# The x mixers of a two-block model in fp32: convolution steps moved ahead, mLSTM decays run two steps ahead instead of one

## The chip, the cores and the metric

The kernel runs on one core of a Trainium2 chip, as one launch. The metric is the device time of one execution in microseconds. The kernel before was run three times: 2325.51, 2322.0 and 2324.71 us, median 2324.71. Engines are called as in the profile: PE (TensorE), DVE (VectorE), ACT (ScalarE), POOL (GpSimd) and SP (SyncE, which issues DMAs).

## What is computed

The reference is a model of two blocks on 256 tokens of width 1024, all in fp32. The first block has forgetting attention and retention, each followed by a mixture of 32 experts. The second block, to which the change belongs, has two layers. In each, a context of 256 tokens and the input x pass a mixer and a feed-forward network. The mixer projects the normed input once and cuts the result into three branches:

```
px = (rmsnorm(x, norm1_g[l]) * (1.0 + sc1) + sh1) @ w_in[l] + b_in[l]
# 1 bidirectional mLSTM, 4 heads of 128, chunks of 128 tokens: q, k, v, o and 16 gate columns
b = cumsum(fc); m_new = max(b_last + m, max(w_log)); decay = exp(b_last + m - m_new)
C_new = decay * C + einsum('bhsk,bhsv->bhkv', ks, vc)
num = w_inter * einsum('bhtk,bhkv->bhtv', qc, C) + einsum('bhts,bhsv->bhtv', s, vc)
h = num / max(abs(den), exp(-m_t))
# 2 chunk_sgu: gelu, layer norm of one half, a product over 128 tokens, times the other half
# 3 conformer_conv: y = a * sigmoid(g); depthwise convolution of 31 taps; layer norm; silu
x = x + g1 * (concat(y_a, y_b, y_c) @ w_out[l])
```

For x the convolution is axial: half of the 256 channels is convolved along rows of 64 tokens (31 taps), the other half along the 4 rows (7 of the taps can reach). Weights are split into a high and a low part, and each product takes three matmuls (high x high, high x low, low x high).

## The kernel before, in words

Every stage is written as one generator or function per engine (`pe`, `act`, `dve`, `pool`, `loads` for SP). Each engine runs its own list in the order written, and engines meet through counted semaphores only. No scheduler moves anything: the order of the work is the order of the code. The stages are attention, experts (with the context's first mixer beside them), retention, experts (with the context's feed-forward network and second mixer beside them), and then twice an x mixer (`x_mixer`, L3268) and an x feed-forward network, and the final norm.

**Items.** `Gemm` (L365) cuts a weight matrix into items of 128 x 1024 numbers. For each, SP loads a slot of the ring, ACT writes `high` (`act_high`, L433), DVE writes `low` (`dve_low`, L444), and PE runs the matmuls (L490). An x mixer has 26 items: two small ones for the gates, then two each for `conv_a`, `conv_g`, `sgu_u` and `sgu_v` (items 2 to 9), and four each for q, k, v and o (10 to 25). There are four pairs of `high` and `low`: ACT and DVE prepare item n + 4 while PE works on n. One 128x1024 low half is the row `DVE L444`.

**What lies between the items.** The generator `dve` (L2951) goes through the items in step (`proj.dve_paced`). From item 4 on it takes `rate` = 4 steps of side work after each low half: first the gate chain (`gate_chain`, L2725: 20 steps on 8 partitions, scans and maxima of the gates), and when that is exhausted the convolution (`conv`, L2781: 43 steps, being a memset, the product a*sigmoid(g), two copies into the padded `yt`, 31 row taps, 7 column taps and a final sum, L2831). In the first x mixer `settle` (L707) follows with nine steps that norm x itself (L710, L715). The SGU's steps on DVE stand after items 10, 11 and 19, its matmuls on PE (L2421, L2426) after item 19.

**The layer norm of the convolution** needs two sums over channels, made on PE with a matrix of ones (`conv_sum_pe`, L2412): one of the values, one of their squares. Between them DVE centres (L2839) and ACT squares (L2584). `ln_at` (L2346) is the item after which the first sum stands on all three engines; the second stands two items later. It is computed from the number of side steps and is 21 before.

**mLSTM.** After the items come four steps i = 0 to 3 (two directions of two chunks; `order`, L2348). For each: PE makes the decays (`decay_pe`) in PSUM, ACT takes their exponential into `wb` (L2602), DVE adds the mask (L2881), ACT takes exponentials of that in place (L2612), DVE multiplies q by `wb` into `qs` (L2894) and the scores by the weights into `mst` or a part of `tm` (L2898), and k into `ks` (L2907). Then `num` (PE L2457 and L2458, DVE L2915 to L2927: the denominators of two heads at a time, and the division) and `state` (PE L2471, DVE L2943), which multiplies the state by one column of `wb` and adds the new product. Numerators and state of step i stand `lag` = `deep` - 1 steps behind its decays; `deep` is 2 for the x mixers (L3270) and 1 for the context's. `deep` also is the number of buffers `wb`, `ks` and `qs`. `Turns` hands out buffers and banks in turn and keeps what frees each. The low halves of the first two items of the output projection stand ahead of the loop's last step (L3016).

Of the kernel before, what the change touches and what calls it, by code (L numbers as in the profile page):

```python
# [15 lines left out]
P = 128  # L16
# [124 lines left out]
def build(nc, A):  # L141
    ctx = ExitStack()
    with ctx:
# [2080 lines left out]
        def mixer(L, v, get, part, room, bk, opened, npairs, wide, rate, deep, early_in=None, x_ready=None, xx=None, rs=None, lender=None):  # L2224
# [42 lines left out]
            kn = part2("kn", 2, 4, P)  # L2267
            if v:
                mod = Modulation(name, room, [(1, 2 if L else 1)], 4 if L else 0, row=kn[:, 0].rearrange("p h d -> p (h d)"), cs=cs)
            wbs, kss = ([part2(n, 4, P) for _ in range(deep)] for n in ("wb", "ks"))  # L2270
            qs_t, st_t, ks_t, wb_t = None, None, Turns(kss, kept), Turns(wbs, kept)
            if not states_only:
                hn = part2("hn", 2, 512)
                qss, sts = [part2("qs", 4, P) for _ in range(deep)], [part2("mst", 4, P)]
                if deep > 1:
                    sts.append(tf[:, 1024:1536].rearrange("p (h t) -> p h t", h=4))
                rd = part2("rd", 4)
                st2.close()
                if v:
                    pairs2 = pairs  # L2280
                    st1.close()
                else:
                    st3, part3 = part()
                    pairs2 = pair_buffers(part3, npairs)
                    st3.close()
                qs_t, st_t = Turns(qss, kept), Turns(sts, kept)
# [56 lines left out]
            x_done = lambda c: [(ev_v, outp.out(0, wide * (c // per), c % per))]  # L2343
            early = Early(f"ffn{L}{v}", xs, T, [ut[:, 0, :], ut[:, 1, :]], x_done) if v else None
            conv_ops, conv_end = 0 if states_only else 43 if v else 65, K("taps") if v else (K("conv"), 65)
            ln_at = (ends["gate"] + 3 + -(-(20 + conv_ops) // rate)) // 2 * 2 + 1  # L2346
            sgu_at, sgu_lag = None if states_only else ends["sgu_v"] + 1, 9 if v else 3
            order = [(0, 0), (1, 1), (0, 1), (1, 0)]  # L2348
            lag = deep - 1
# [534 lines left out]
            def prelude_dve(dve, i):  # L2884
                d, a = order[i]
                le = P - 1 if d == 0 else 0
                s0, s1 = a * P, (a + 1) * P
                dt, wb = dts[i % 2], wb_t[K(i)]
                if i in outs:
                    qs, st = qs_t.next(K(i)), st_t.next(K(i))  # L2890
                    for s, k in qs_t.freed(K(i)):
                        dve.wait_ge(*s.at(k))
                    dve.wait_ge(*pl_a.at(K(i, 1)))
                    dve.tensor_tensor(qs, qt[:, :, s0:s1], wb, MUL).then_inc(*qs_v.up(K(i)))  # L2894
                    wb_t.free(K(i), (qs_v, K(i)))
                    dve.wait_ge(*ms_p.at(K(i)))
                    dve.wait_ge(*pd_a.at(K(i, 1)))
                    dve.tensor_tensor(st, bk[K("mscore", i)][:, :].rearrange("p (h t) -> p h t", h=4), dt, MUL).then_inc(*ms_v.up(K(i)))  # L2898
                    bk.free(K("mscore", i), (ms_v, K(i)))
                if i not in final:  # L2900
                    ks = ks_t.next(K(i))
                    for s, k in ks_t.freed(K(i)):
                        dve.wait_ge(*s.at(k))
                    dve.wait_ge(*pd_a.at(K(i, 1)))
                    if i < 2:
                        dve.wait_ge(*kn_a.at(K(1)))
                    dve.tensor_tensor(ks, kn[:, a], bc(dt[:, :, le], [P, 4, P], 2), MUL).then_inc(*ks_v.up(K(i)))  # L2907

            def num_dve(dve, i, hp):
                d, a = order[i]  # L2910
                pv = bk[K("num", i, hp)][:, 0:258].rearrange("p (h n) -> p h n", h=2)
                em = emt[:, 8 * d + 4 * a + 2 * hp:8 * d + 4 * a + 2 * hp + 2]
                seq = in_order(dve, v_step, K("den", i, hp))
                dve.wait_ge(*mo_p.at(K(i, hp)))
                seq(dve.tensor_copy(rd[:, 2:4], pv[:, :, 128]))  # L2915
                if i < 2:
                    dve.wait_ge(*gt_a.at(K(1, "m")))
                seq(dve.scalar_tensor_tensor(rd[:, 0:2], rd[:, 2:4], -1.0, em, MUL, MAX))
                seq(dve.tensor_tensor(rd[:, 0:2], rd[:, 0:2], rd[:, 2:4], MAX))
                seq(dve.reciprocal(rd[:, 0:2], rd[:, 0:2]))  # L2920
                for j in range(2):
                    h = 2 * hp + j
                    o = hn[:, a, h * P:(h + 1) * P]
                    if i >= 2:
                        n = dve.scalar_tensor_tensor(o, pv[:, j, 0:P], rd[:, j:j + 1], o, MUL, ADD)
                    else:
                        n = dve.tensor_scalar(o, pv[:, j, 0:P], rd[:, j:j + 1], None, MUL)  # L2927
                n.then_inc(*mo_v.up(K(i, hp)))
                dve.wait_ge(*mo_v.at(K(i, hp)))
                bk.free(K("num", i, hp), (mo_v, K(i, hp)))  # L2930

            def state_dve(dve, i, hp):
                d, a = order[i]
                le = P - 1 if d == 0 else 0
                wb = wb_t[K(i)]
                pv = bk[K("state", i, hp)][:, 0:258].rearrange("p (h n) -> p h n", h=2)
                dve.wait_ge(*mc_p.at(K(i, hp)))
                dve.wait_ge(*pl_a.at(K(i, hp)))
                if i < 2 and hp == 0:
                    dve.wait_ge(*cn_v.at(state_before(i)))  # L2940
                for j in range(2):
                    h = 2 * hp + j
                    n = dve.scalar_tensor_tensor(cn[:, d, h, :], cn[:, d, h, :], wb[:, h, le:le + 1], pv[:, j, :], MUL, ADD)  # L2943
                n.then_inc(*cn_v.up(K(i, hp)))
                bk.free(K("state", i, hp), (cn_v, K(i, hp)))
                if hp:
                    wb_t.free(K(i), (cn_v, K(i, 1)))

            sq4 = None if states_only else [qss[0], sts[0]]
# [1 line left out]
            def dve(dve):  # L2951
# [21 lines left out]
                    yield  # L2973
                    yield from norm_turns(lambda part: norm.split_dve(dve, None, part))
                yield
                chains, taps = gate_chain(dve), iter(())
                for it in proj.dve_paced(dve):
                    if it is None:
                        yield
# [2 lines left out]
                    if mod and L and at == 6:  # L2982
                        mod.out_dve(dve, 1, 2)
                    if at > ends["gate"] + 2:
                        for _ in range(rate):
                            if chains is not None and next(chains, True):
                                chains, taps = None, iter(()) if states_only else conv(dve)
                            if chains is None and next(taps, True):
                                next(settle, None)
                    if not states_only:  # L2990
# [6 lines left out]
                        if at in (ln_at, ln_at + 2):  # L2997
                            conv_ln_dve(dve, (at - ln_at) // 2)
                    yield
                run(chains or taps)  # L3000
                run(settle)
                for which in late():
                    conv_ln_dve(dve, which)
# [263 lines left out]

        def x_mixer(L, before, opened, early_in, x_ready):  # L3268
            room = Room(f"mix{L}", 8, before, opened)
            early, x_done, s = mixer(L, 1, room, room.part, room, banks, opened, 4, 512, 4, 2, early_in, x_ready)  # L3270
            room.close()
            return room, early, x_done, in_one_go(s)

# [242 lines left out]
```

## Time and profile before

| | |
|---|---|
| median of 3 runs | 2324.71 us |
| the profiled execution | 2330.65 us |
| its span in the profile | 2328.7 us |
| mean granted clock of PE | 0.955 |
| PE busy | 2133.0 us, 92% |
| DVE busy | 1118.6 us, 48% |
| ACT busy | 870.9 us, 37% |
| DMA | 676.24 MB, mean 290 GB/s |

The profiled execution is one more run, 5.9 us above the median; 2.0 us of it lie outside the span. Everything read from the trace is on the clock of its span. Busy shares are means over stages with different limits, so the change is read where it happens: the first x mixer's projections end near 1689 us and its mLSTM near 1723 us, the second's near 2054 and 2088 us. A wait in brackets is idle time of the engine just before the instruction, with what ended it.

### The profile page before, as it was taken

The page shows a single profiled execution, that of the slowest core. Times are in us where ns is not written, and L with a number is a line of the kernel's source. Part 1 is how long each engine was busy: PE and PEld are TensorE (multiplying, and loading weights), DVE is VectorE, ACT ScalarE, POOL GpSimd, SP SyncE. Part 2 cuts the span into 40 slices and gives each one's busy share as a digit, 9 for nine tenths or more (in the row PEclk, how much of TensorE's full clock was granted, in tenths as well). Part 3 has the DMA queues.
Part 4 walks back from the last instruction along what each step waited for, and adds up shares of the span by engine and source line. Part 5 has one row for each costly group of instructions (what it writes and reads, how often), then busy time and mean ns, then how long its engine had stood idle before and what let it go on. Part 6 is the DMA issues. An engine that isn't in the chain of part 4 may idle for free. (4 is left out here: it accounts for less than half of the span.)

```text
span 2328.7 us, 44642 instructions
## 1 busy us (share of the span) xinstructions
PE 2133.0 (92%) x19242; PEld 1728.9 (74%) x19242; DVE 1118.6 (48%) x1956; ACT 870.9 (37%) x1473; POOL 83.7 (4%) x160
## 2 busy tenths in 40 slices
PE   7998889998786999989999998977989999988999
PEld 7967556665553987967777776636878998878999
DVE  5455326533523743543433335324865545765554
ACT  4434233243212443332322222324444444554443
POOL 0000000000000000001010110000000000000001
PEclk9989999999998999999999999998989999988999
DMA  8567999999999568599999999897426556513550
GB/s 296 163 236 282 382 412 417 381 387 425 424 426 374 177 227 302 212 383 417 409 391 408 422 411 376 358 412 285 157 92 247 185 166 210 179 55 135 184 177 31
DMA packets 128078, 676.24 MB, mean 290 GB/s; under 512 B 11488, under 2 KB 11744, under 8 KB 65920
## 3 DMA queue, kind: packets, MB, share of 16 engines
q1 hardware_dynamic: 111616, 614.77, 67.8%
q0 software_dynamic: 16256, 58.50, 6.6%
q8 instruction: 157, 2.57, 0.4%
q14 instruction: 49, 0.40, 0.0%
HBM read 672.17 MB, written 1.05 MB: 289 GB/s over the span
## 5 line engine op out<-in xcount | busy, mean ns | idle before, releaser
L490 PE MATMUL bank<-xx,high 128*128 128x256 f32 (+1 forms) x3296 | 630.8, 293 | 30.2 <-DVE xx L653 13.7
L490 PEld LDWEIGHTS bank<-xx,high 128*128 128x128 f32 (+1 forms) x3296 | 518.5, 194 | 90.5 <-issue 61.3
L490 PE MATMUL bank<-xx,low 128*128 128x256 f32 (+1 forms) x1648 | 473.4, 287 | 0.0
L490 PEld LDWEIGHTS bank<-xx,low 128*128 128x128 f32 (+1 forms) x1648 | 319.9, 194 | 1.0
L444 DVE TENSOR_TENSOR low<-lane,high 128x1024 fp32r<-128x1024 f32 (+1 forms) x112 | 130.7, 1170 | 256.6 <-ACT high L433 256.4
L433 ACT ACTIVATE high<-lane 128x1024 fp32r<-128x1024 f32 (+1 forms) x112 | 113.1, 1013 | 288.0 <-PE bank L490 284.1
L490 PE MATMUL bank<-hx,high 128*128 128x256 f32 x1056 | 197.4, 288 | 0.0
L490 PEld LDWEIGHTS bank<-hx,high 128*128 128x128 f32 x1056 | 163.9, 191 | 18.1 <-issue 16.0
L490 PE MATMUL bank<-hx,low 128*128 128x256 f32 x528 | 149.2, 283 | 0.0
L490 PE MATMUL bank<-gth,high 128*128 128x256 f32 x384 | 112.9, 294 | 6.6 <-DVE gtl L651 5.2
L1484 ACT ACTIVATE hs<-bank 64x256 f32<-64x256 f32 x64 | 24.1, 377 | 246.6 <-PE bank L1471 246.2
L490 PE MATMUL bank<-gth,low 128*128 128x256 f32 x384 | 110.7, 288 | 0.0
L490 PE MATMUL bank<-gtl,high 128*128 128x256 f32 x384 | 110.6, 288 | 0.0
L490 PE MATMUL bank<-high,xx 128*128 128x256 f32 (+1 forms) x416 | 103.9, 330 | 0.7 <-DVE tm L2839 0.7
L1491 DVE TENSOR_TENSOR hs<-hs,bank 64x256 f32<-64x256 f32 x64 | 27.1, 423 | 154.9 <-ACT hs L1484 154.5
L490 PEld LDWEIGHTS bank<-hx,low 128*128 128x128 f32 x528 | 101.0, 191 | 0.0
L490 PEld LDWEIGHTS bank<-gth,high 128*128 128x128 f32 x384 | 75.7, 197 | 13.3 <-DVE low L444 7.2
L1540 DVE COPY y<-bank 128x256 f32<-128x256 f32 x64 | 27.1, 423 | 121.5 <-PE bank L1525 121.1
L444 DVE TENSOR_TENSOR low<-ring__14,high 128x1024 fp32r<-128x1024 f32 x50 | 60.8, 1222 | 50.5 <-ACT high L433 50.2
L490 PEld LDWEIGHTS bank<-high,xx 128*128 128x128 f32 x416 | 71.4, 191 | 17.5 <-issue 8.8
L490 PE MATMUL bank<-xh,high 128*128 128x256 f32 x256 | 74.8, 292 | 7.0 <-DVE low L444 3.5
L1552 PE MATMUL bank<-tmp,y 32*128 32x256 f32 x1024 | 78.9, 424 | 1.5 <-DVEq L1641 1.1
(602 smaller groups left out, 3977.4 us busy)
## 6 DMA issues: line engine op xcount, KB each, us to landing
ring__13<-in_expert_gu_blocks SPq DMA_DIRECT2D x36, 1024.0 KB, 10.4
ring__14<-in_expert_gu_blocks SPq DMA_DIRECT2D x35, 1024.0 KB, 9.6
ring__15<-in_expert_gu_blocks SPq DMA_DIRECT2D x35, 1024.0 KB, 9.8
lane<-in_w_gu_blocks POOLq DMA_DIRECT2D x44, 512.0 KB, 8.5
ring__47<-in_expert_gu_blocks SPq DMA_DIRECT2D x18, 1024.0 KB, 11.9
ring__159<-in_expert_gu_blocks SPq DMA_DIRECT2D x18, 1024.0 KB, 9.6
ring__160<-in_expert_gu_blocks SPq DMA_DIRECT2D x18, 1024.0 KB, 9.3
ring__158<-in_expert_gu_blocks SPq DMA_DIRECT2D x18, 1024.0 KB, 9.8
```

Source lines behind the costliest of these rows:

```text
L433: act.activation(self.split_parts(it)[0].bitcast(F32R), src, ACT.Copy).then_inc(*hi.up(it["key"]))
L444: dve.tensor_tensor(low.bitcast(F32R), src, high, SUB).then_inc(*lo.up(it["key"]))
L490: done = pe.matmul(out, a.bitcast(F32R), b.bitcast(F32R), start=it["start"] and k == 0 and q == 0 and (not halves or u == it["outs"][0]), ...
L1484: act.activation(hs[0:64, :], pq[K("up", b)][0:64, 0:256], ACT.Silu).then_inc(*up_a.up(K(b)))
L1491: dve.tensor_tensor(hs[0:64, :], hs[0:64, :], pq[K("up", b)][64:128, 0:256], MUL).then_inc(*up_v.up(K(b)))
L1540: dve.tensor_copy(y, pq[key][:, 0:256]).then_inc(*dn_v.up(K(b)))
L1552: i = pe.matmul(acc_b[h][:, j * T:(j + 1) * T], y[32 * h:32 * h + 32, j * P:(j + 1) * P], d[32 * h:32 * h + 32, b % GB, :], start=False, s ...
```

## The change

Two things, both in `mixer`, for the x mixers (v = 1).

**The convolution starts beside the gate chain.** As soon as item 5, the last of `conv_g`, is past, every second one of DVE's four side steps is followed by one convolution step, though the gate chain isn't through. Six convolution steps so come before item 9 instead of from item 9 on. `ln_at` is computed with the six steps taken off and becomes 19: the two sums stand after items 19 and 21.

**The decays run two steps ahead.** `deep` is 3 and `lag` 2. There are three `qs` and three places for the weighted scores (the third is a part of `tm`, which the SGU no longer needs by then), but still two `wb` and two `ks`. For steps 0 and 1 the last column of `wb` is copied to a small `wle` right after `qs` is made; the state update reads `wle`, and `wb` is free after the copy. In all mixers, the context's too, the denominators aren't copied from PSUM any more; the two steps behind read them there.

```diff
-            wbs, kss = ([part2(n, 4, P) for _ in range(deep)] for n in ("wb", "ks"))
+            wbs, kss = ([part2(n, 4, P) for _ in range(min(deep, 2))] for n in ("wb", "ks"))
+            wle = part2("wle", 2, 4) if v else None
...
-                    sts.append(tf[:, 1024:1536].rearrange("p (h t) -> p h t", h=4))
+                    sts += [tf[:, z:z + 512].rearrange("p (h t) -> p h t", h=4) for z in (1024, 1536)]
...
-            ln_at = (ends["gate"] + 3 + -(-(20 + conv_ops) // rate)) // 2 * 2 + 1
+            early_taps = 2 * (ends["gate"] + 3 + 20 // rate - ends["conv_g"] - 1) if v else 0
+            ln_at = (ends["gate"] + 3 + -(-(20 + conv_ops - early_taps) // rate)) // 2 * 2 + 1
...
                     wb_t.free(K(i), (qs_v, K(i)))
+                    if v and i not in final:
+                        dve.tensor_copy(wle[:, i, :], wb[:, :, le]).then_inc(*qs_v.up(K(i, "last")))
+                        wb_t.free(K(i), (qs_v, K(i, "last")))
...
-                seq(dve.tensor_copy(rd[:, 2:4], pv[:, :, 128]))
...
-                seq(dve.scalar_tensor_tensor(rd[:, 0:2], rd[:, 2:4], -1.0, em, MUL, MAX))
-                seq(dve.tensor_tensor(rd[:, 0:2], rd[:, 0:2], rd[:, 2:4], MAX))
+                seq(dve.scalar_tensor_tensor(rd[:, 0:2], pv[:, :, 128], -1.0, em, MUL, MAX))
+                seq(dve.tensor_tensor(rd[:, 0:2], rd[:, 0:2], pv[:, :, 128], MAX))
...
-                dve.wait_ge(*pl_a.at(K(i, hp)))
+                dve.wait_ge(*(qs_v.at(K(i, "last")) if v else pl_a.at(K(i, hp))))
...
-                    n = dve.scalar_tensor_tensor(cn[:, d, h, :], cn[:, d, h, :], wb[:, h, le:le + 1], pv[:, j, :], MUL, ADD)
+                    n = dve.scalar_tensor_tensor(cn[:, d, h, :], cn[:, d, h, :], wle[:, i, h:h + 1] if v else wb[:, h, le:le + 1], pv[:, j, :], MUL, ADD)
...
-                if hp:
+                if hp and not v:
                     wb_t.free(K(i), (cn_v, K(i, 1)))
...
-                chains, taps = gate_chain(dve), iter(())
+                chains, taps = gate_chain(dve), conv(dve) if v else iter(())
...
-                        for _ in range(rate):
-                            if chains is not None and next(chains, True):
-                                chains, taps = None, iter(()) if states_only else conv(dve)
+                        for n in range(rate):
+                            if chains is not None:
+                                if next(chains, True):
+                                    chains, taps = None, taps if v else iter(()) if states_only else conv(dve)
+                                elif v and at > ends["conv_g"] and n % 2:
+                                    next(taps)
...
-            early, x_done, s = mixer(L, 1, room, room.part, room, banks, opened, 4, 512, 4, 2, early_in, x_ready)
+            early, x_done, s = mixer(L, 1, room, room.part, room, banks, opened, 4, 512, 4, 3, early_in, x_ready)
```

In the rows below, line numbers of the changed kernel are two to eight higher, and ring buffers have other numbers.

The first sum of the layer norm on PE, second x mixer, before: L493 is the bias that closes a group of v, L2412 the sum.

```order
L490 MATMUL bank<-high,xx 128x512
L493 MATMUL bank<-row,ones_r 128x512
L2412 MATMUL bank<-tm,vec 128x256 x2
L490 MATMUL bank<-high,xx 128x512
L490 MATMUL bank<-low,xx 128x512
L490 MATMUL bank<-high,xx 128x512 x2
```

And now: L2428 are the last matmuls of the SGU, L2414 is the sum.

```order
L2423 MATMUL bank<-row,vec 64x256 x2
L2428 MATMUL bank<-wst,tm 64x128 x4
L2423 MATMUL bank<-row,vec 64x256 x2
L2428 MATMUL bank<-wst,tm 64x128 x4
L2414 MATMUL bank<-tm,vec 128x256 x2
L490 MATMUL bank<-high,xx 128x512
L490 MATMUL bank<-low,xx 128x512
```

The sum stood behind the last v item; now it stands right behind the SGU's matmuls, with the last two v items still to come.

The end of the convolution on DVE, second x mixer, before: L444 are the low halves of items 22 and 23, L2814 and L2825 taps, L2831 the final sum, L2872 the SGU's product.

```order
L2814 SCALAR_TENSOR_TENSOR tm<-yt,vec,tm 128x256
L444 TENSOR_TENSOR low<-ring__301,high 128x1024
L2814 SCALAR_TENSOR_TENSOR hn<-yt,vec,hn 128x256
L2814 SCALAR_TENSOR_TENSOR tm<-yt,vec,tm 128x256
L2831 TENSOR_TENSOR tm<-tm,hn 128x256
L2872 TENSOR_TENSOR yt<-tm,bank 128x256 x2
L444 TENSOR_TENSOR low<-ring__300,high 128x1024 x2
L2839 SCALAR_TENSOR_TENSOR tm<-bank,tm 128x256 x2
L2844 RECIPROCAL rs<-rs 128x256
L2846 TENSOR_TENSOR tm<-tm,rs 128x512
```

And now, with L2833 as the final sum, ring__303 for items 22 and 23, and L2841 as the centring:

```order
L2816 SCALAR_TENSOR_TENSOR hn<-yt,vec,hn 128x256
L2816 SCALAR_TENSOR_TENSOR tm<-yt,vec,tm 128x256
L2816 SCALAR_TENSOR_TENSOR hn<-yt,vec,hn 128x256
L2816 SCALAR_TENSOR_TENSOR tm<-yt,vec,tm 128x256
L444 TENSOR_TENSOR low<-ring__303,high 128x1024
L2833 TENSOR_TENSOR tm<-tm,hn 128x256
L444 TENSOR_TENSOR low<-ring__303,high 128x1024
L2874 TENSOR_TENSOR yt<-tm,bank 128x256 x2
L2841 SCALAR_TENSOR_TENSOR tm<-bank,tm 128x256 x2
L444 TENSOR_TENSOR low<-ring__302,high 128x1024 x2
```

The final sum stands behind the low half of item 22 instead of item 23, and the centring ahead of the low half of item 24.

The second half of the mLSTM's step 1 on DVE, second x mixer, before: `rd` are the denominators.

```order
L2881 TENSOR_TENSOR tm<-bank,vec 128x256 x2
L2894 TENSOR_TENSOR qs<-qt,wb 128x512
L2898 TENSOR_TENSOR tm<-bank,tm 128x512
L2907 TENSOR_TENSOR ks<-kn,tm 128x512
L2915 COPY rd<-bank 128x2
L2918 SCALAR_TENSOR_TENSOR rd<-rd,rs 128x2
L2919 TENSOR_TENSOR rd<-rd 128x2
L2920 RECIPROCAL rd<-rd 128x2
```

And now:

```order
L2883 TENSOR_TENSOR tm<-bank,vec 128x256 x2
L2896 TENSOR_TENSOR qs<-qt,wb 128x512
L2899 COPY wle<-wb 128x4
L2903 TENSOR_TENSOR tm<-bank,tm 128x512
L2912 TENSOR_TENSOR ks<-kn,tm 128x512
L2883 TENSOR_TENSOR tm<-bank,vec 128x256 x2
L2896 TENSOR_TENSOR qs<-qt,wb 128x512
L2903 TENSOR_TENSOR tm<-bank,tm 128x512
L2922 SCALAR_TENSOR_TENSOR rd<-bank,rs 128x2
```

The mask and products of step 2 (L2883, L2896, L2903) stand between those of step 1 and the numerators of step 0, and the copy ahead of the denominators is gone.

## Rows read from the trace of the kernel before

**Rows 1.** The page, its line on PE: busy us (share) and instructions.

```profile
PE 2133.0 (92%) x19242; PEld 1728.9 (74%) x19242; DVE 1118.6 (48%) x1956; ACT 870.9 (37%) x1473; POOL 83.7 (4%) x160
```

**Rows 2.** Table of stretches: length, busy us per engine, PE clock, DMA share, GB/s.

```profile
1626.00:1671.00 45.00, 44.74 (x321) 39.88 (x320) 42.72 (x85) 23.27 (x32) 0.00 (x0) 1.00 0.51 165
1680.85:1684.26 3.41, 3.41 (x10) 2.66 (x9) 1.88 (x2) 1.76 (x2) 0.00 (x0) 0.50 0.27 109
1695.25:1723.18 27.93, 23.23 (x149) 21.69 (x149) 23.65 (x77) 12.49 (x30) 0.00 (x0) 0.83 0.07 18
1994.20:2039.53 45.33, 44.52 (x324) 39.46 (x322) 43.10 (x88) 23.10 (x31) 0.00 (x0) 1.00 0.53 166
2059.83:2087.76 27.93, 23.02 (x148) 21.57 (x147) 23.60 (x77) 12.49 (x30) 0.00 (x0) 0.82 0.07 19
```

**Rows 3.** Timeline of PE, first x mixer: start, us, what [wait before <- releaser].

```profile
1664.03 0.66 PE L2426 MATMUL bank<-wst,tm 128*64 128x128 f32 x8
...
1671.36 1.13 PE L2412 MATMUL bank<-tm,vec 128*128 128x256 f32 x4
...
1680.29 1.51 PE L2412 MATMUL bank<-tm,vec 128*128 128x256 f32 x4 [2.34 <-ACT tm L2584]
```

**Rows 4.** Timeline of PE, second x mixer.

```profile
2019.29 0.51 PE L490 MATMUL bank<-xx,high 128*128 128x256 f32 x2 [0.81 <-DVE low L444]
...
2032.49 0.66 PE L2426 MATMUL bank<-wst,tm 128*64 128x128 f32 x8
...
2039.91 1.13 PE L2412 MATMUL bank<-tm,vec 128*128 128x256 f32 x4
...
2046.47 1.02 PE L2412 MATMUL bank<-tm,vec 128*128 128x256 f32 x4
```

**Rows 5.** Timeline of DVE, second x mixer, projections.

```profile
1994.20 1.23 DVE L444 TENSOR_TENSOR low<-ring__300,high 128x1024 fp32r<-128x1024 f32 x1 [5.40 <-ACT high L433]
...
2005.94 0.91 DVE L2787 MEMSET yt<- 128x1016 f32 x1 [0.16 <-issue]
...
2012.99 1.23 DVE L444 TENSOR_TENSOR low<-ring__14,high 128x1024 fp32r<-128x1024 f32 x1 [1.31 <-ACT high L433]
...
2018.02 1.22 DVE L444 TENSOR_TENSOR low<-ring__15,high 128x1024 fp32r<-128x1024 f32 x1
2019.15 0.48 DVE L2825 SCALAR_TENSOR_TENSOR tm<-yt,vec,tm 128x256 f32<-128x256 f32 x1
2019.55 0.48 DVE L2814 SCALAR_TENSOR_TENSOR hn<-yt,vec,hn 128x256 f32<-128x256 f32 x1
...
2039.10 0.43 DVE L2831 TENSOR_TENSOR tm<-tm,hn 128x256 f32<-128x256 f32 x1
```

**Rows 6.** Timeline of DVE, first x mixer, the convolution's end and what follows.

```profile
1670.69 0.42 DVE L2831 TENSOR_TENSOR tm<-tm,hn 128x256 f32<-128x256 f32 x1
1671.03 1.75 DVE L710 RECIPROCAL on<-on 128x256 f32<-128x256 f32 x1
...
1674.43 1.67 DVE L715 SCALAR_TENSOR_TENSOR xr<-xr,vec,on 128x256 f32<-128x256 f32 x4
...
1678.73 0.74 DVE L2839 SCALAR_TENSOR_TENSOR tm<-bank,tm 128x256 f32<-128x256 f32 x2
```

**Rows 7.** Timeline of DVE, second x mixer, mLSTM.

```profile
2061.66 0.69 DVE L2898 TENSOR_TENSOR mst<-bank,tm 128x512 f32<-128x512 f32 x1 [0.48 <-ACT tm L2612]
...
2065.91 0.15 DVE L2915 COPY rd<-bank 128x2 f32<-128x2 f32 x1
2066.10 0.16 DVE L2918 SCALAR_TENSOR_TENSOR rd<-rd,rs 128x2 f32<-128x2 f32 x1
...
2070.39 0.76 DVE L2881 TENSOR_TENSOR tm<-bank,vec 128x256 f32<-128x256 f32 x2 [0.50 <-ACT wb L2602]
```

**Rows 8.** Timeline of PE behind the mLSTM, first and second x mixer.

```profile
1719.32 0.51 PE L490 MATMUL bank<-xx,high 128*128 128x256 f32 x2 [0.47 <-DVE low L444]
...
2091.93 0.63 PE L2557 MATMUL bank<-vec,hn 128*128 128x128 f32 x4 [2.11 <-DVE hn L3051]
```

More of the change, by code:

```diff
@@ L2934, in state_dve @@
                 le = P - 1 if d == 0 else 0
-                wb = wb_t[K(i)]
+                wb = None if v else wb_t[K(i)]
                 pv = bk[K("state", i, hp)][:, 0:258].rearrange("p (h n) -> p h n", h=2)
                 dve.wait_ge(*mc_p.at(K(i, hp)))
-                dve.wait_ge(*pl_a.at(K(i, hp)))
+                dve.wait_ge(*(qs_v.at(K(i, "last")) if v else pl_a.at(K(i, hp))))
                 if i < 2 and hp == 0:
@@ L2999, in dve @@
                     yield
-                run(chains or taps)
+                run(chains or ())
+                run(taps)
                 run(settle)
```

## The prediction

> **What bounds the kernel now.** I read the page's head first. PE is busy for 92% of the span, so a wait removed elsewhere pays only where PE was standing for it [rows 1]. The change touches the two x mixers. The table of stretches separates two phases in each of them, together 73 of the 2329 us. In the projections PE is busy 44.7 of 45.0 us and 44.5 of 45.3 us, DVE 42.7 and 43.1: both engines are full at once, PE ahead by a hair. In the mLSTM stretches (27.9 us each) PE is busy 23 us, DVE 23.6, the clock is granted at 0.82, and DVE's order sets the end [rows 2].
>
> Then PE's timeline, to see where it stood. In the first mixer it waited 2.34 us for the second sum of the convolution's layer norm at 1680.29 [rows 3]; right behind that the granted clock was 0.5 for 3.41 us [rows 2], which cost half of it, 1.7 us. In the second mixer it waited 0.81 us at 2019.29, and neither of the two sums (L2412) shows a wait [rows 4]. So the second mixer's projections have almost nothing to give.
>
> DVE's timeline shows why. In the second mixer it is idle for 5.40 us before 1994.20, which is before the convolution's inputs exist, then only 0.16 us before the memset and 1.31 us before 2012.99 until the convolution ends at 2039.10 + 0.43 = 2039.53 [rows 5]. PE's first sum starts 0.38 us later, at 2039.91 [rows 4]. In the first mixer the same pair is 1671.11 and 1671.36 [rows 3, 6]. The end of the convolution already meets the sum.
>
> **Part 1, the convolution beside the gate chain.** Nothing is added or removed on DVE. Six of the 43 steps (memset, product, two copies, two taps) move ahead of three low halves, and everything behind runs six steps earlier in items. But DVE is already full there, so its clock time hardly moves. Of the work ahead of the convolution's end only one low half drops out (the last but two in the projections): 1.13 us by the spacing 2018.02 to 2019.15 [rows 5]. Besides, the memset's 0.16 us goes, and steps put between dependent gate steps overlap: dependent ones start 0.04 us after the end of the one before (2065.91 to 2066.10, with 0.15 us of work) [rows 7], independent ones 0.09 us before it (2018.02 to 2019.15, with 1.22 us of work) [rows 5]. Some four crossings at 0.13 us give 0.5, with the memset's 0.16 about 0.6 (bounds 0 and 1.2). So the end of the convolution comes 1.7 us earlier: 2037.8 and 1669.4. The 1.31 us stays, since ACT still has to wait for DVE's statistics.
>
> On PE the sums move two items forward, from item 21 to 19 and from 23 to 21. Two items that stood ahead of the first sum now stand behind it: from the end of the SGU matmuls to the sum, 2039.91 - (2032.49 + 0.66) = 6.76 us, in the first mixer 1671.36 - (1664.03 + 0.66) = 6.67 us [rows 3, 4]. Second mixer: the sum starts 2.1 us earlier with 6.76 us more behind it, so the projections end 6.76 - 2.1 = 4.7 us later. First mixer: 6.67 - 1.95 = 4.7 us later, less the 2.34 us wait and the 1.7 us of slow clock, since the second sum's input is then ready: convolution end 1669.4, plus one low half (1.1), the reciprocal (1.7), six steps of L715 (2.4), the gated product and the centring (0.7 each) and ACT's square (0.7 with its hand-over), 7.3 us [rows 5, 6], gives 1676.7, and PE is there at 1669.4 + 0.8 + 6.7 = 1676.9. Rest 4.7 - 4.0 = 0.7 us.
>
> Where does the wait show? Six taps of 0.40 us now precede the low half of item 16, less 0.6: it lands 1.8 us late, PE starts that item at 2021.1 instead of 2019.3, and it reaches the first sum at 2033.15 + 1.8 = 2034.95, where it stands 2.85 us (first mixer: 1666.4 to 1669.4, 3.0 us). Waits of 2 to 3 us can cost clock, as the 2.34 us one did; the 0.81 us one did not. A drop at the first of the two waits is absorbed by the second, one at the second is paid. Between 0 and 1.7 us in each mixer, 3.4 if it lasts twice as long; I take 0.8, for two 1.6.
>
> **Part 2, decays two steps ahead.** In each mixer DVE waits twice 0.50 us for ACT's `wb`, which waits for the buffer that the state update still reads [rows 7]; the copied column frees it, and the decay matmuls now stand ahead of the numerators on PE. Gain 1.0 us. The waits of 0.48 us for ACT's exponentials (four per mixer) stay, as DVE still has only the `qs` product between asking and needing. The two new copies (like L2915, 0.15 us) fall into these waits: cost 0; 0.3 if not. The copy of the denominators goes: eight times 0.19 us by the spacing of 2065.91 and 2066.10, 1.5 us [rows 7]. Sum 2.5 us per mixer (bounds 1.0 and 2.9).
>
> Does PE see it? In the second mixer its transposes wait 2.11 us for `hn` [rows 8], so yes. In the first they wait for nothing, but follow two output items and the modulation; those items start on the low halves at 1719.32 with 0.47 us of waiting [rows 8], and these low halves move from behind numerator 2 to ahead of it, so they come more than 2.5 us earlier. Yes there too. Two mixers: -5.0 us.
>
> The two steps that replace the denominators' copy now read PSUM. The row of such a read is 0.15 us, of the same size from SBUF 0.16 us [rows 7]: I add nothing, and 0.02 us each for 16 is the bound, 0.3 per mixer. The Trainium skill (VectorE: DVE Perf Modes, "Rules for kernel authors") says to copy out of PSUM first if many steps follow, and its table in the section on the TRN2 errata gives 120 cycles fixed for a PSUM source against 58 for SBUF. At its 0.96 GHz that is an estimate of 65 ns more on each of the 16 steps, 1.0 us per mixer, and by it the total would be 2.0 us slower. The rows speak against it: at 128x2 the PSUM read is the shorter.
>
> In the context mixer, beside the experts, the same eight copies go; DVE is not what that stage waits for, and I count 0.
>
> **Sum.** First mixer +0.7 - 2.5, second +4.7 - 2.5, clock +1.6: +2.0 us. The profiled execution took 2330.65 us; it becomes 2332.7. The median of the runs is 5.9 us below that execution, and 2324.71 + 2.0 = 2326.7 us.
>
> **Rivals.** The measurement tells apart about 0.2%, 4.65 us.
> (a) Forecast: the two parts nearly cancel; from -3 to +4.6 us. 56%.
> (b) The clock pays. Both waits at the first sum are followed by one or two spells of 0.5, 1.7 to 3.4 us each instead of 0.8, and the mLSTM keeps only 2 us per mixer: 5.4 + 3.4 to 6.8 - 4 = +4.8 to +8.2, 2331 to 2332. For it: the 2.34 us wait did so. Against: a first drop absorbs into the wait that follows. 25%.
> (c) Faster. The convolution's end comes as early as PE does. It decides at 3 us: the gate chain would have to hide the six steps in its own dependencies, so that the low halves are not late and the end moves from 1.7 to 5 us earlier. Then the second mixer's projections stay as they were, the first loses its 4.0 us, and with 5.0 from the mLSTM it is -9, 2315.7 us. For it: gate steps are on 8 partitions and short; against it: they start 0.04 us behind each other, there is no room. Half of that shift gives -4.5. With both 13%.
> (d) Part 2 does not do what it says: a bank or buffer wait stands in for `wb`, only the denominators' copies are gained, 1.5 per mixer, less with slower PSUM reads. +2.0 + 2.0 to +4.0, 2329 to 2331. For it: eight banks now serve one more step in flight. Against it: each bank asked for was read a whole step earlier. 6%.
>
> **How the numbers follow.** Faster by over 0.2%: (c) less its nearer half, 0.11. Slower: (b), half of (d) and the upper tail of (a), 0.31. Within 0.2%: 0.58. The range leaves out the end of (c) and the top of (b): 2318.5 to 2332.5; that of (a) alone is 2321.7 to 2329.3.
>
> **What would show it.** Right: PE idle of some 3 us ahead of the first layer-norm sum in both mixers, released by DVE's last convolution step; PE idle of 2 us at item 16; no wait at the second sum; DVE's end of convolution only 1 to 2 us earlier from the start of the projections; no wait for `wb` at decays 2 and 3, 25.4 us instead of 27.9 for the mLSTM on DVE. Wrong: a first sum without a wait (then (c)), short steps on PSUM above 0.2 us, or DVE idle in the gate stretch.

## The result, and the profile after

The changed kernel took 2329.35 us (median of 15 runs) against 2323.42 us for the kernel before (15 runs on the same chip): a ratio of 1.0021, 95% interval 1.0014 to 1.0029, so +3.3 to +6.7 us. (Each kernel had one far slower run, 2428.99 and 3356.71 us; the ratio is over the others, while the medians, over all runs, are 5.9 us apart.) A second comparison, on another occasion (below, the changed kernel again), gave 1.0014 (1.0004 to 1.0024). The forecast was +2.0 us, 2326.7 us: the right side of zero, but below the first interval. The change is slower, by about as much as a measurement can just tell.

The profiled execution after took 2324.49 us, with a span of 2322.7 us. That is shorter than the profiled execution before, though the medians stand the other way: the stages ahead of the x mixers, which the change hardly touches, differed by 8.7 us between the two executions (the x mixers start at 1630.8 us before and at 1622.1 after). So below only stretches between fixed points are compared, and from the start of the first x mixer's SGU projections to the end of the span it is 697.9 us before and 700.6 after.

The page's line on engines, to be read against [rows 1]: eight copies in each x mixer and eight more in the context's are gone, and four new ones are there (DVE has 1936 instructions where it had 1956). PE has the same instructions.

```profile
PE 2122.5 (91%) x19242; PEld 1723.4 (74%) x19242; DVE 1113.9 (48%) x1936; ACT 870.6 (37%) x1473; POOL 83.9 (4%) x160
```

The table below has, in us and from the timelines, what the stretches of the x mixers took, and what lies behind them. "Projections" runs from PE's first bias matmul of `sgu_v` to its first transpose of k, "mLSTM" from there to the first transpose of `hn`.

| | before | after | forecast |
|---|---|---|---|
| projections, first x mixer | 59.41 | 61.87 | +0.7, and clock |
| mLSTM, first | 38.58 | 34.46 | -2.5 |
| projections, second x mixer | 55.76 | 62.10 | +4.7, and clock |
| mLSTM, second | 37.10 | 34.35 | -2.5 |
| behind the first mLSTM, up to the second mixer's projections | 270.2 | 269.6 | nothing |
| behind the second mLSTM, up to the end of the span | 236.8 | 238.1 | nothing |
| end of the convolution after item 10's low half | 43.03 and 43.34 | 41.49 and 41.79 | -1.7 |

PE's timeline after, first x mixer (start, us, what, and in brackets the wait before it and its releaser), answers to [rows 3]:

```profile
1639.30 0.50 PE L490 MATMUL bank<-xx,high 128*128 128x256 f32 x2 [1.00 <-ACT qt L2301]
...
1644.27 0.50 PE L490 MATMUL bank<-xx,high 128*128 128x256 f32 x2 [1.12 <-DVE low L444]
...
1661.01 1.57 PE L2414 MATMUL bank<-tm,vec 128*128 128x256 f32 x4 [2.93 <-DVE tm L2833]
...
1670.22 1.13 PE L2414 MATMUL bank<-tm,vec 128*128 128x256 f32 x4
```

The same of the second x mixer, which answers to [rows 4]:

```profile
2005.12 0.50 PE L490 MATMUL bank<-xx,high 128*128 128x256 f32 x2 [0.42 <-DVE low L444]
...
2010.13 0.50 PE L490 MATMUL bank<-xx,high 128*128 128x256 f32 x2 [2.03 <-DVE low L444]
...
2023.33 0.66 PE L2428 MATMUL bank<-wst,tm 128*64 128x128 f32 x8
...
2026.88 2.04 PE L2414 MATMUL bank<-tm,vec 128*128 128x256 f32 x4 [2.89 <-DVE tm L2833]
...
2036.11 1.13 PE L2414 MATMUL bank<-tm,vec 128*128 128x256 f32 x4
```

In both mixers PE stands for the first sum, 2.93 and 2.89 us, and the second sum has no wait. The four matmuls of the first sum take 1.57 and 2.04 us, where those of the second take 1.13: the clock has fallen. The table of stretches after (columns as in [rows 2]) shows that, for the stretch right behind each of the two waits, and then the mLSTM of the second mixer:

```profile
1661.50:1664.90 3.40, 3.40 (x9) 2.68 (x8) 3.36 (x6) 0.00 (x0) 0.00 (x0) 0.50 0.15 60
2026.75:2030.10 3.35, 3.22 (x8) 2.59 (x9) 2.53 (x5) 0.35 (x1) 0.00 (x0) 0.50 0.71 203
2055.17:2080.35 25.18, 23.77 (x162) 22.45 (x162) 22.24 (x71) 12.36 (x30) 0.00 (x0) 0.82 0.13 44
```

The granted clock is 0.50 over 3.4 us, as it was behind the one wait of 2.34 us before. DVE's timeline after, second x mixer, for [rows 5]:

```profile
1984.94 1.19 DVE L444 TENSOR_TENSOR low<-ring__301,high 128x1024 fp32r<-128x1024 f32 x1
...
1987.30 0.91 DVE L2789 MEMSET yt<- 128x1016 f32 x1 [0.16 <-DVE gM L2760]
...
2003.84 1.23 DVE L444 TENSOR_TENSOR low<-ring__14,high 128x1024 fp32r<-128x1024 f32 x1 [1.31 <-ACT high L433]
...
2008.86 1.22 DVE L444 TENSOR_TENSOR low<-ring__15,high 128x1024 fp32r<-128x1024 f32 x1
...
2026.32 0.41 DVE L2833 TENSOR_TENSOR tm<-tm,hn 128x256 f32<-128x256 f32 x1
```

The wait of 1.31 us is still there and DVE is as full as before. The convolution ends at 2026.32 + 0.41 = 2026.73, 41.79 us behind the start of item 10's low half at 1984.94. That is the next one behind the low half that ended the long idle time. Before, the same low half starts at 1996.19, and it was 2039.53 - 1996.19 = 43.34.

In the mLSTM, DVE's timeline (second x mixer) answers to [rows 7]:

```profile
2056.44 0.16 DVE L2899 COPY wle<-wb 128x4 f32<-128x4 f32 x1
2057.01 0.69 DVE L2903 TENSOR_TENSOR mst<-bank,tm 128x512 f32<-128x512 f32 x1 [0.41 <-ACT tm L2614]
...
2063.70 0.15 DVE L2922 SCALAR_TENSOR_TENSOR rd<-bank,rs 128x2 f32<-128x2 f32 x1
2063.88 0.16 DVE L2923 TENSOR_TENSOR rd<-rd,bank 128x2 f32<-128x2 f32 x1
...
2067.24 0.74 DVE L2883 TENSOR_TENSOR tm<-bank,vec 128x256 f32<-128x256 f32 x2
...
2080.35 0.69 DVE L3046 TENSOR_TENSOR mst<-hn 128x512 f32<-128x512 f32 x1
```

The mask of the last step (2067.24) has no wait for `wb` any more. The new copy lies inside the wait for ACT's exponentials, which is 0.41 us where it was 0.48. The short steps that read PSUM take 0.15 and 0.16 us. From the first mask to L3046 DVE needs 25.18 us, 2.75 less than before.

PE behind the mLSTM of the second mixer, for [rows 8]:

```profile
2084.52 0.88 PE L2559 MATMUL bank<-vec,hn 128*128 128x128 f32 x4 [3.45 <-DVE hn L3059]
```

PE's wait for `hn` has grown from 2.11 to 3.45 us, since the output items that PE does ahead of it start earlier, and the transposes behind it take 0.88 us instead of 0.63: the clock has fallen behind this wait too. From these transposes to the next output item it is 4.64 us (2084.52 to 2089.16), where before it was 4.18 (2091.93 to 2096.11). The whole stretch behind takes 1.4 us more, and its granted clock is lower, as the table of stretches shows before and after:

```profile
2091.93:2328.70 236.77, 222.38 (x1792) 219.62 (x1792) 122.91 (x158) 105.87 (x158) 12.01 (x14) 0.97 0.39 130
```

```profile
2084.52:2322.65 238.13, 223.94 (x1792) 220.87 (x1792) 122.88 (x158) 105.89 (x158) 12.01 (x14) 0.95 0.38 129
```

### The profile page after: what moved, and what is told of

Its sections match the earlier page's. It is cut to its first block and busy times, and to the rows that moved or that the text cites. A ratio compares the mean times of both kernels' runs of the same rounds, so it can differ in the third digit from the quotient of the medians.

```text
span 2322.7 us, 44621 instructions
## 1 busy us (share of the span) xinstructions
PE 2122.5 (91%) x19242; PEld 1723.4 (74%) x19242; DVE 1113.9 (48%) x1936; ACT 870.6 (37%) x1473; POOL 83.9 (4%) x160
## 5 line engine op out<-in xcount | busy, mean ns | idle before, releaser
L444 DVE TENSOR_TENSOR low<-lane,high 128x1024 fp32r<-128x1024 f32 (+1 forms) x112 | 130.7, 1170 | 253.8 <-ACT high L433 253.6
L444 DVE TENSOR_TENSOR low<-ring__14,high 128x1024 fp32r<-128x1024 f32 x50 | 60.8, 1223 | 50.5 <-ACT high L433 50.2
```

The lines of the kernel that those rows point to most:

```text
L444: dve.tensor_tensor(low.bitcast(F32R), src, high, SUB).then_inc(*lo.up(it["key"]))
```

## The experiments

Ratios are against the kernel before on the same chip, with 95% intervals. The edits are shown cut short; "..." marks what is left out.

**1. Part 1 alone.** The convolution's early steps and `ln_at` 19; the mLSTM as before.

```
  before, plus (...):
+ early_taps = 2 * (ends["gate"] + 3 + 20 // rate - ends["conv_g"] - 1) if v else 0
+ chains, taps = gate_chain(dve), conv(dve) if v else iter(())
+                elif v and at > ends["conv_g"] and n % 2: next(taps)
```

> Part 1 alone: the convolution beside the gate chain and the two sums at items 19 and 21, everything of the mLSTM as before. Theory A (DVE is full, so the sum stands for the convolution's end): PE waits 2.9 us at the first sum in both mixers, the projections end about 2.5 us later in the first and 6.3 us later in the second (what the changed kernel's trace shows between fixed points), and the whole is 8 to 10 us slower than before, ratio 1.0034 to 1.0043. Rival B (the two parts disturb each other, each alone is harmless): within 3 us of before. Rival C (the loss of the changed kernel lies outside the projections): 0 to 3 us slower and no 2.9 us waits.

Measured: 1.0028 (1.0018 to 1.0038), +6.5 us. The projections took 61.86 and 62.30 us, the mLSTM 38.56 and 37.07 us: all of the loss is there, none of the gain. The projections came out as expected, the total did not: 1.0028 is less than the 1.0034 to 1.0043 that was expected, though its interval reaches into that range. PE's table of waits in the first x mixer's last 60 us (engine, tile, line, releaser: us in total, times, longest):

```profile
PE bank L2413 <- DVE tm L2832: 2.9, 1, 2.9
PE bank L490 <- DVE low L444: 1.1, 1, 1.1
PE bank L490 <- ACT qt L2300: 1.0, 1, 1.0
PE bank L2515 <- ACT on L2315: 0.7, 1, 0.7
```

And its timeline at the first sum of the second:

```profile
2035.21 2.04 PE L2413 MATMUL bank<-tm,vec 128*128 128x256 f32 x4 [3.12 <-DVE tm L2832]
```

The waits and the slow first sum belong to part 1 and don't need part 2.

**2. Part 2 alone.** `deep` 3, `lag` 2, `wle`, no copy of the denominators; the convolution behind the gate chain, `ln_at` 21.

```
  changed kernel, but (...):
- chains, taps = gate_chain(dve), conv(dve) if v else iter(())
+ chains, taps = gate_chain(dve), iter(())
```

> Part 2 alone: decays two steps ahead, column copy, no copy of the denominators; convolution and sums as before. Theory A: 2.5 to 2.8 us less per mixer on DVE, all of it seen by PE, total 4 to 6.5 us faster, ratio 0.9972 to 0.9983. Rival B (the gain is given back behind the mLSTM, at the clock or at the output projection): within 2 us of before though DVE's stretch is 2.7 us shorter. Rival C (reading PSUM twice is dear): stretch shorter by at most 1.7 us, short steps over 0.2 us.

Measured: 0.9973 (0.9960 to 0.9986), -6.3 us. The mLSTM took 34.49 and 34.36 us, the projections 59.42 and 55.53. DVE's masks of steps 0, 2 and 3 in the second mixer, and the end:

```profile
2050.34 0.76 DVE L2882 TENSOR_TENSOR tm<-bank,vec 128x256 f32<-128x256 f32 x2 [1.52 <-ACT wb L2603]
...
2056.43 0.75 DVE L2882 TENSOR_TENSOR tm<-bank,vec 128x256 f32<-128x256 f32 x2
...
2062.42 0.75 DVE L2882 TENSOR_TENSOR tm<-bank,vec 128x256 f32<-128x256 f32 x2
...
2075.53 0.69 DVE L3041 TENSOR_TENSOR mst<-hn 128x512 f32<-128x512 f32 x1
```

**3 and 4. Part 2 taken apart.** Experiment 3 is the kernel before without the copy of the denominators; experiment 4 is part 2 alone with that copy left in.

```
  experiment 3 (experiment 4 has these three the other way round):
- seq(dve.tensor_copy(rd[:, 2:4], pv[:, :, 128]))
- seq(dve.scalar_tensor_tensor(rd[:, 0:2], rd[:, 2:4], -1.0, em, MUL, MAX))
+ seq(dve.scalar_tensor_tensor(rd[:, 0:2], pv[:, :, 128], -1.0, em, MUL, MAX))
```

> Only the copy of the denominators goes, in all three mixers that have it, one step of lag as before. Theory A: DVE's mLSTM stretch 1.5 us shorter in each x mixer, total 2 to 3 us faster (0.9987 to 0.9992), the context's mixer gives nothing. Rival C (PSUM reads 65 ns longer each): stretch 0.5 us shorter, total within 1 us.

> Two steps of lag and the column copy, but the denominators are still copied. Theory A: the two waits of 0.50 us for ACT go in each mixer, the low halves of the output projection come ahead of numerator 2, stretch 1.0 us shorter, total 2 to 3.5 us faster (0.9985 to 0.9991). Rival D (a bank wait takes the place of the wb wait): stretch as before, total within 1 us.

Measured: 0.9990 (0.9979 to 1.0001) and 0.9990 (0.9978 to 1.0002). Neither can be told from no change by its time alone; the trace tells more. DVE in experiment 3, second mixer, masks of steps 0 and 3 and the end:

```profile
2048.89 0.76 DVE L2881 TENSOR_TENSOR tm<-bank,vec 128x256 f32<-128x256 f32 x2 [1.52 <-ACT wb L2602]
...
2059.06 0.76 DVE L2881 TENSOR_TENSOR tm<-bank,vec 128x256 f32<-128x256 f32 x2 [0.50 <-ACT wb L2602]
...
2075.21 0.69 DVE L3037 TENSOR_TENSOR mst<-hn 128x512 f32<-128x512 f32 x1
```

In experiment 4, step 3 and the end (its mask of step 0 starts at 2052.07):

```profile
2064.74 0.75 DVE L2882 TENSOR_TENSOR tm<-bank,vec 128x256 f32<-128x256 f32 x2
...
2079.06 0.69 DVE L3042 TENSOR_TENSOR mst<-hn 128x512 f32<-128x512 f32 x1
```

From the first mask to the end that is 2075.21 - 2048.89 = 26.32 us with the 0.50 us wait still there, and 2079.06 - 2052.07 = 26.99 us without it; before it is 27.93, with both 25.19. So the copies are worth 1.6 us in this mixer (1.8 where the second step ahead is already there), the second step ahead 0.9 us (1.1 without the copies), and both together 2.7. Rival (d) is out: the waits for `wb` at steps 2 and 3 are gone and no other stands in for them. So is the estimate worked out from the Trainium skill (VectorE: DVE Perf Modes, the table in the section on the TRN2 errata): by it experiment 3 would have lost 1.0 us of its 1.5 on the PSUM reads; it gained 1.6.

**5 and 6. The changed kernel again, and with the sums put back.** Experiment 5 is the changed kernel as it stands. Experiment 6 keeps the early convolution steps but counts `ln_at` as before, so the sums stand after items 21 and 23.

```
  experiment 6:
- ln_at = (ends["gate"] + 3 + -(-(20 + conv_ops - early_taps) // rate)) // 2 * 2 + 1
+ ln_at = (ends["gate"] + 3 + -(-(20 + conv_ops) // rate)) // 2 * 2 + 1
```

> The changed kernel once more beside the others of this call. Part 1 alone was 1.0028 of before (1.0018 to 1.0038) and part 2 alone 0.9973 (0.9960 to 0.9986), product 1.0001, while the changed kernel was 1.0021 (1.0014 to 1.0029). Theory A (the parts add; the gap is scatter of the interval ends): 1.0003 to 1.0020, between fixed points of the trace the x stages 0 to 4 us longer than before. Rival (the parts cost something only together): again 1.0021 or more, and a wait in the trace that neither part alone shows.

> The changed kernel with the two layer-norm sums (and centring and square) back at items 21 and 23; the six early convolution steps stay. Theory A: no wait at the first sum; the late low half of item 16 stays as the only cost, so the second mixer's projections take 57.3 to 57.9 us (before 55.8, changed 62.1) and the first's 59 to 61 (before 59.4, changed 61.9), total 0.9978 to 0.9990 of before. Rival (the early steps themselves are what costs, through low halves of all items): second mixer's projections over 60 us and the total as the changed kernel's.

Measured: 1.0014 (1.0004 to 1.0024) for the changed kernel, 0.9978 (0.9967 to 0.9989) with the sums put back. PE's waits in experiment 6, first and then second mixer:

```profile
PE bank L490 <- DVE low L444: 1.1, 1, 1.1
PE bank L490 <- ACT qt L2301: 1.0, 1, 1.0
PE bank L2515 <- ACT on L2316: 0.7, 1, 0.7
...
PE bank L490 <- DVE low L444: 2.4, 2, 1.9
PE bank L2515 <- ACT on L2316: 0.7, 1, 0.7
```

The waits at items 15 and 16 stay (late low halves), those at the sums are gone, and the projections take 57.58 us in both. Moving the two sums forward by two items therefore costs 4.3 us in the first mixer and 4.5 in the second. The early steps as such cost the second mixer 57.58 - 55.53 = 2.0 us against experiment 2 (the forecast's low half 1.8 us late) and give the first 1.8, since the wait for the second sum is gone. The expectation missed that gain: it had 59 to 61 us for the first mixer.

The mLSTM of its first mixer was 36.03 us, not 34.46. There the clock fell early in it, as the table of stretches shows (columns as in [rows 2]):

```profile
1687.20:1700.90 13.70, 13.70 (x58) 12.56 (x59) 9.34 (x24) 8.20 (x26) 0.00 (x0) 0.51 0.00 1
```

And DVE waited for the numerators of step 0, as its timeline shows at their denominators:

```profile
1699.62 0.16 DVE L2921 SCALAR_TENSOR_TENSOR rd<-bank,rs 128x2 f32<-128x2 f32 x1 [1.03 <-PE bank L2459]
```

Every mLSTM begins with such a spell, of 7 to 10 us in the other traces of this case; this one began earlier and lasted longer, and why isn't known. Even with it the kernel is the second fastest of the first six.

**7. Part 2 alone, and x's own norm later.** If the 2.34 us wait of [rows 3] comes from the nine steps of x's norm that DVE puts between the convolution and the second sum's input, these steps can stand behind `ln_at`, and no early convolution is needed.

```
- if chains is None and next(taps, True):
+ if chains is None and next(taps, True) and at > ln_at:
      next(settle, None)
```

> Part 2 alone, and the nine steps that norm x itself (first mixer) wait until the centring is past. Theory A: the centring comes some 4.9 us earlier, PE's 2.3 us wait at the second sum goes and with it up to 1.7 us of slow clock, first mixer's projections 55.5 to 57.1 us instead of 59.4, second's unchanged at 55.5 to 55.8; total 0.9956 to 0.9968 of before, the fastest kernel of all. Rival (the next thing late is the eviction of o, which waits for x): first mixer's projections over 58.5 us and a wait of ACT for L715.

Measured: 0.9951 (0.9938 to 0.9965), 2314.53 us against 2325.07: the fastest of all, and a little better than the 0.9956 to 0.9968 expected. PE's timeline in its first mixer, the two sums and k's transposes:

```profile
1666.00 1.13 PE L2413 MATMUL bank<-tm,vec 128*128 128x256 f32 x4
...
1672.42 1.03 PE L2413 MATMUL bank<-tm,vec 128*128 128x256 f32 x4
...
1680.69 1.10 PE L2515 MATMUL bank<-vec,kt 128*128 128x128 f32 x8 [0.69 <-ACT on L2316]
```

Neither sum waits, the clock stays up behind them, and the first mixer's projections take 55.23 us, 4.2 less than before: the 2.34 us and 1.7 us of clock that the forecast gave to that wait, 4.0 together.

**8. Fewer taps.** The changed kernel with its row convolution cut from 31 to 23 taps, so that the convolution ends before PE is at the first sum (the last eight row taps and the last column tap, and their part of the result, are left out: nine steps of DVE).

```
- for k in range(31):
+ for k in range(23):
...
- dve.wait_ge(*conv_v.at(K("tap", 30)))
+ dve.wait_ge(*conv_v.at(K("tap", 22)))
```

> The changed kernel, but the last eight of the 31 row taps and the last of the seven column taps of the x mixers' convolutions are left out, 9 steps of 0.40 us on DVE; nothing else moves. Theory A (the first sum waits for a full DVE): the convolution ends 3.6 us earlier, the 2.9 us waits at the first sum are gone or under 0.3 us, the late item 16 stays, second mixer's projections 57.3 to 59.2 us, first's 57 to 60. Rival (the wait is for something else, such as ACT or a bank): waits at the first sum over 1.5 us.

One run, 2320.51 us. The projections took 57.29 and 57.65 us, as in experiment 6. PE at the two sums of the second mixer:

```profile
2026.05 1.13 PE L2414 MATMUL bank<-tm,vec 128*128 128x256 f32 x4
...
2033.76 1.13 PE L2414 MATMUL bank<-tm,vec 128*128 128x256 f32 x4
```

With the sums where the change puts them but their input early, the loss is gone: the place of the sums costs nothing by itself, only the wait does, 62.10 - 57.65 = 4.5 us, of which 2.89 is the wait and the rest, 1.6, clock.

**9. Sums after items 20 and 22.** The changed kernel with both sums one item later.

```
- ...early_taps) // rate)) // 2 * 2 + 1
+ ...early_taps) // rate)) // 2 * 2 + (2 if v else 1)
```

> The changed kernel with the two sums one item later, at 20 and 22. Theory A (the first sum may stand no earlier than the convolution's end; PE has 3.4 us of item 20 to fill the 2.9 us wait): no wait at the first sum in the second mixer, its projections 57.3 to 58.0 us as with the sums at 21 and 23; in the first mixer a wait of 1 to 3 us at the second sum, since the centring now stands behind one more low half and two more settle steps; total 0.9978 to 0.9995 of before. Rival (every place ahead of 21 costs): waits at both sums, second mixer over 60 us.

Measured: 0.9976 (0.9964 to 0.9988). PE at the two sums of the first mixer:

```profile
1665.43 1.10 PE L2414 MATMUL bank<-tm,vec 128*128 128x256 f32 x4
...
1675.04 1.13 PE L2414 MATMUL bank<-tm,vec 128*128 128x256 f32 x4 [1.74 <-ACT vn L2306]
```

One item's delay does away with the wait of the first sum. In the second mixer, which has no x norm of its own, there is no wait at either sum, and the projections take 57.75 us. In the first mixer the second sum waits 1.74 us, but its matmuls run at full speed (1.13 us), and the projections take 59.58 us.

**10. The kernel before, and x's own norm later.** The edit of experiment 7 on the kernel before.

> The kernel before with one thing changed: the nine steps that norm x itself wait until the centring is past. Theory A: the first mixer's projections 55.2 to 55.6 us instead of 59.4 (the 2.3 us wait at the second sum and 1.7 us of slow clock), nothing else changed, total 0.9975 to 0.9990 of before, and this times part 2 alone (0.9973) is the kernel with both (0.9951). Rival (only together with part 2 does it pay): within 1 us of before.

Measured: 0.9967 (0.9955 to 0.9980). The first mixer's projections took 55.22 us, the second's 55.75, the mLSTM 38.60 and 37.10: only the wait for the second sum and its clock are gone. The total fell by more than the 0.9975 to 0.9990 that was expected, -4.7 to -10.5 us by the interval. From the first projections to the end the trace gives -7.0 us, 4.2 of it in the mixers and 2.8 behind them, where the edit changes nothing. So this edit gives 4.2 us in the mixer's trace with or without part 2, and what part 1 took away in the first mixer (the wait for the second sum) was to be had without it.

## Why the prediction was right, and where it was off

The waits came out where and as long as forecast, and the parts nearly cancel, as in (a). But the clock was wrong twice, with opposite signs, and a part of the loss lies behind the mixers, for which the forecast had nothing. The measured +4.9 us (the ratio's) lies just above (a), which ends at +4.6, and at the lower edge of (b), which begins at +4.8; the interval, +3.3 to +6.7, covers parts of both. Of (b) the clock came true, one spell of 1.7 us in each mixer, but not that the mLSTM would keep only 2 us per mixer. (The prediction wrote (b) down as 2331 to 2332 us; its own terms give 2329.5 to 2332.9.)

**End of the convolution 1.7 us earlier.** Measured 1.55 in both mixers. Right: the six early steps push three low halves behind them, DVE stays full.

**A wait of 3.0 and 2.85 us at the first sum, none at the second.** Measured 2.93 and 2.89, and none. Experiment 8 shows that it is this wait that costs.

**Item 16's low half 1.8 us late.** PE waited 2.03 us there in the second mixer and 0.42 at item 15, and experiment 6 prices it at 2.0. In the first mixer the wait splits, 1.00 us for ACT's eviction of q at item 15 and 1.12 for the low half; the first of these was not foreseen. It moved no end, since the first sum's input was the later.

**The clock: 1.6 us in all.** This term was mis-sized. It was 1.7 us in each mixer, 3.4 in all. The argument was that a fall of the clock at the first of two waits is absorbed by the second. But the waits at items 15 and 16, up to 2.03 us, were followed by no fall; the fall came behind the first sum, in both mixers of all three traces with that wait (after, and experiments 1 and 5), where nothing stood behind it to absorb it. With 1.7 each the forecast of the projections is +2.4 and +6.4 us, and measured are +2.46 and +6.34.

**The mLSTM: -2.5 us in each.** DVE gained 2.75 in the second mixer, as experiments 3 and 4 split it: 1.6 to 1.8 for the copies and 0.9 to 1.1 for the waits. In the first mixer the stretch on PE gained 4.1, of which 2.4 is as forecast: the last step's numerators start 1.95 us earlier (23.18 us behind k's transposes, where it was 25.13), and the wait of 0.47 us for the low half is gone. The other 1.7 us is clock, which was not foreseen: a second slow spell near the end of the mLSTM is gone (last section). From the start of these numerators to the first output item it is 1.78 us (1707.17 to 1708.95), and 3.94 before (1715.38 to 1719.32, with the 0.47 in it). Experiment 4 separates the two: there PE doesn't wait for the low half either, but the second spell is there, and the numerators take 3.39 us (1709.69 to 1713.08).

**The sum.** The four stretches of the mixers give 2.46 + 6.34 - 4.12 - 2.75 = +1.9 us. That this is the forecast's +2.0 is luck: the clock took 1.8 us more than forecast at the sums and gave back 1.7 in the first mLSTM. With the clock at 3.4 and all else as it stands, the forecast's terms would give 0.7 + 4.7 + 3.4 - 5.0 = +3.8 us, which lies in both measured intervals, +3.3 to +6.7 and +0.9 to +5.6, but isn't how the time came about.

**Behind the mixers: nothing.** The stretch behind the second mLSTM grew by 1.4 us, of which 0.46 lies between the transposes and the next output item. Behind the longer wait for `hn` the clock is slow for 10.2 us, where it was 6.8 before. This isn't the scatter of one trace: in four traces (after, and experiments 2, 5 and 7) the stretch takes 238.0 to 238.2 us with the clock at 0.50 for 23 us of it, in the other eight 236.0 to 237.1 us with 10 to 17 us of slow clock. Why just these four is open. It isn't the wait alone: experiments 6, 8 and 9 have part 2 and the same wait of 3.45 us, and take 236.4 to 236.6 us. Behind the first mLSTM the profiled kernel before took 270.2 us, the longest of all twelve traces (267.3 to 269.6 in the others), so its span hides a part of the loss.

**What stays open.** The parts apart give 1.0028 x 0.9973 = 1.0001, the whole 1.0021 and 1.0014. The intervals overlap, but the whole is the slower in both comparisons. In the traces the stretch from the first projections to the end is +6.7 for part 1 and -7.6 for part 2, against +2.7 for both. Inside the mixers the parts add up: +8.9 and -7.1, and +1.9 for both. The gap lies behind the mixers, in stretches that neither part edits: -2.2 and -0.5, and +0.7 for both (+0.6 in experiment 5). There the clock is at 0.50 for 34.2 us before, 27.3 with part 1, 36.5 with part 2 and 40.0 with both. So the gap goes with the clock; what sets these spells is not settled, and each number is one trace's, in which such a stretch scatters by 1 to 2 us.

## What to carry to other kernels

When work of a full engine is only put in another order, the end of the chain moves by what drops out ahead of it (here 1.55 us), while a consumer that is moved with it moves by whole items (here 6.7 us): ask for both, and keep the consumer behind its input. Price a PE wait of the size that was followed by a slow spell here (2.3 to 3.1 us, in dense work) at the wait plus the clock behind it; that was 4.5 us for 2.9. Look at the clock behind the edited stretch too. And look for what delays the producer that is waited for: putting the nine steps in its way behind it (experiments 7 and 10) was worth more than starting it early.

## What the runs showed of the hardware

- Behind a PE wait of 2.33 or 2.34 us (before, experiments 2 to 4), 2.89 to 2.93 and 3.12 us (after, experiments 1 and 5) at a sum, the granted clock was 0.50 for 3.4 us each time, ten of ten, 1.7 us lost. Behind 1.74, 2.03 and the pair of 1.00 and 1.12 us there was no such fall at the items that followed.
- The slow clock of the mLSTM is two spells in the kernel before and in experiments 1, 3, 4 and 10, one at its beginning and one some 25 us behind k's transposes, and only the first where the decays run two steps ahead without the copies (after, and experiments 2 and 5 to 9). The second, in the table of stretches (columns as in [rows 2]) of before and then the same place after:

```profile
2078.60:2085.40 6.80, 5.05 (x28) 4.79 (x29) 5.89 (x19) 5.73 (x8) 0.00 (x0) 0.75 0.00 1
```

```profile
2074.00:2080.80 6.80, 6.80 (x61) 6.80 (x59) 6.25 (x23) 0.71 (x3) 0.00 (x0) 1.00 0.47 157
```

- Two steps on a 128x2 tile that read PSUM took 0.15 and 0.16 us, no more than from SBUF (0.16), and started 0.18 us apart.
- A copy of 0.15 us ahead of dependent steps cost 0.20 us: eight of them, 1.6 us.
